# The second feed-forward's input product as seven block products of 256 columns

## The reference

```python
def swiglu(h, w_in, w_out):
    gate, up = jnp.split(h @ w_in, 2, axis=-1)
    return (jax.nn.silu(gate) * up) @ w_out
...
x = x + g2 * swiglu(rms_norm(x, norm_ffn[i]) * (1.0 + sc2) + sh2, ffn_w_in[i], ffn_w_out[i])
```

## Time and profile before

| | us |
|---|---|
| median of the 3 runs shown (2650.46 to 2651.87) | 2650.99 |
| span of the profiled execution | 2648.4 |
| TensorE busy in the span | 2524.9 |
| VectorE, ScalarE, GpSimd busy | 1580.9, 1163.8, 776.8 |
| second feed-forward, from the first full token low part to the end | 2293 to 2648 |

### The profile page before, as it was taken

One profiled execution on the slowest core, in us unless ns is written; L12 is line 12 of the kernel. 1 busy time (PEld: TensorE's weight loads), 2 busy tenths in 40 slices (PEclk: granted clock), 3 DMA queues, 4 the chain that ended last, 5 costly groups with the idle time before them and its releaser, 6 DMA issues.

```text
span 2648.4 us, 41072 instructions
## 1 busy us (share of the span) xinstructions
PE 2524.9 (95%) x15450; PEld 2240.3 (85%) x15450; DVE 1580.9 (60%) x2588; ACT 1163.8 (44%) x2142; POOL 776.8 (29%) x466
## 2 busy tenths in 40 slices
...
GB/s 278 133 143 143 141 174 206 32 70 63 103 96 17 120 76 29 93 122 95 146 142 128 137 87 114 165 101 134 256 205 124 111 33 80 66 98 99 102 96 79
DMA packets 124352, 307.19 MB, mean 116 GB/s; under 512 B 12448, under 2 KB 38048, under 8 KB 122784
## 3 DMA queue, kind: packets, MB, share of 16 engines
...
## 4 chain that ended last, share of the span: by engine, by line
PE 77%; DVE 10%; ACT 5%; issue 5%; POOL 2%; DMA 1%; SPq 0%; ACTq 0%; DVEq 0%; POOLq 0%
PE ps L568 15%; PE ps L570 15%; PE ps L569 15%; PE ps L1627 4%; PE ps L1629 3%; PE ps L1628 3%; PE ps L1522 3%; PE ps L1498 2%; PE ps L1508 2%; ACT prb L2306 1%; PE ps L1402 1%; PE ps L1404 1%; PE ps L1403 1%; PE ps L897 1%; PE ps L936 1%
## 5 line engine op out<-in xcount | busy, mean ns | idle before, releaser
L549 POOL TENSOR_TENSOR Wl<-raws,Wh 128x2048 fp32r<-128x2048 f32 (+3 forms) x82 | 318.6, 3886 | 1200.2 <-ACT Wh L543 1191.3
L568 PE MATMUL ps<-Hh,Wh 128*128 128x384 f32 (+2 forms) x1088 | 375.6, 345 | 6.4 <-DVE xT L3315 2.8
L570 PE MATMUL ps<-Hh,Wl 128*128 128x384 f32 (+2 forms) x1088 | 370.4, 340 | 0.0
L569 PE MATMUL ps<-Hl,Wh 128*128 128x384 f32 (+2 forms) x1088 | 370.3, 340 | 0.0
L543 ACT ACTIVATE Wh<-raws 128x2048 fp32r<-128x2048 f32 (+3 forms) x125 | 204.8, 1639 | 180.2 <-PE ps L570 140.4
L3304 DVE SCALAR_TENSOR_TENSOR xT<-ps,mod,xT 128x384 f32<-128x384 f32 (+3 forms) x174 | 84.5, 533 | 277.8 <-PE ps L570 277.8
L568 PEld LDWEIGHTS ps<-Hh,Wh 128*128 128x128 f32 x1088 | 205.2, 189 | 15.3 <-issue 4.9
L569 PEld LDWEIGHTS ps<-Hl,Wh 128*128 128x128 f32 x1088 | 205.3, 189 | 6.4 <-issue 1.9
L570 PEld LDWEIGHTS ps<-Hh,Wl 128*128 128x128 f32 x1088 | 205.1, 189 | 4.9
L2969 DVE SCALAR_TENSOR_TENSOR ybuf<-ubuf,vec,ybuf 128x770 f32<-128x770 f32 x144 | 155.5, 1080 | 55.1 <-ACT ybuf L1824 40.5
L568 PE MATMUL ps<-H1h,Wh 128*128 128x512 f32 (+1 forms) x368 | 141.7, 385 | 4.5 <-DVE H1l L2844 3.4
...
## 6 DMA issues: line engine op xcount, KB each, us to landing
raws<-in_slabs SPq DMA_DIRECT2D x218, 512.0 KB, 4.6
adl<-in_ada ACTq DMA_DIRECT2D x48, 512.0 KB, 3.6
ada<-in_ada SPq DMA_DIRECT2D x32, 512.0 KB, 3.9
...
ada<-in_ada SPq DMA_DIRECT2D x8, 1024.0 KB, 11.3
...
```

Of the source, the lines that this page charges most:

```text
L549: nc.gpsimd.tensor_tensor(Wl[n % 2][:, 0:w], raw[n % 2][:, 0:w], Wh[n % 2][:, 0:w].bitcast(f32), ALU.subtract).then_inc(sig("slab_lo"), 1)
L568: nc.tensor.matmul(o, lhs(c)[0], rhs(c, t0, t1)[0], start=(s == 0), stop=False)
L569: nc.tensor.matmul(o, lhs(c)[0], rhs(c, t0, t1)[1], start=False, stop=False)
L570: last = nc.tensor.matmul(o, lhs(c)[1], rhs(c, t0, t1)[0], start=False, stop=(s == k - 1))
```

## The change

For chunks 2 to 21 of the second feed-forward the input product takes the seven-product form. The weight slab is cut into quarters: feature blocks 0 to 3 or 4 to 7, gate or up columns. The tokens are cut likewise: feature blocks, and tokens 0 to 255 or 256 to 511. VectorE forms three sums of weight quarters in the tile `gone` and a difference in place (`dve_sums7`), and once the token sums (`dve_tokens7`). A product of the seven is 4 feature blocks x 3 = 12 matmuls on 256 columns. Four of the additions that join the products are left to PSUM: a later product goes on accumulating on a bank that holds an earlier one (`BANK7`; `FRESH7` names the products that start a bank anew). ScalarE copies the state of a bank out before the next product adds to it (`w7_copy`), and VectorE adds gate and up quarters from these copies and from PSUM. Of the seven pieces' low parts GpSimd takes 0, 4, 5 and 6, VectorE 1, 2 and 3. The pieces of one slab fill both slots of `Wh` and `Wl` (0 to 3 in one, 4 to 6 in the other), so each piece of the next slab is written when its predecessor's product is done. Chunks 0 and 1 stay as they were. The loops are written out.

```diff
+        BANK7 = (0, 1, 0, 1, 0, 2, 0)
+        FRESH7 = (0, 1, 5)
...
+        def piece7(t, q):
+            return by_k(t[EVEN7 if q < 4 else 1 - EVEN7][:, 512 * (q % 4):512 * (q % 4) + 512])
...
+        def pe_seven1(pe, grp):
...
+            for y, (x, s, n, c) in enumerate(slabs7(grp)):
+                for q in range(7):
+                    if q in (0, 4, 5):
+                        pe.wait_ge(sig("w7_lo"), past("w7_lo") + 3 * x + (0, 4, 5).index(q) + 1)
+                    elif q < 4:
+                        pe.wait_ge(sig("w7_low"), past("w7_low") + 3 * x + q)
+                    else:
+                        slab_ready(pe, n, 0)
+                    if q == 0 and y == 0:
+                        pe.wait_ge(sig("gemm_evac0"), u0 + s + 1)
+                    if q == 5 and y == 0:
+                        pe.wait_ge(sig("gemm_evac1"), u0 + s + 1)
...
+                    if x == 0 and q in (1, 2, 4, 6):
+                        pe.wait_ge(sig("u7_lo"), past("u7_lo") + (4 if q == 6 else 3))
+                    if q in (2, 3, 4):
+                        pe.wait_ge(sig("w7_copy"), past("w7_copy") + 3 * x + q - 1)
+                    if q == 6:
+                        pe.wait_ge(sig("w7_up"), past("w7_up") + x + 1)
+                    h, l, o = piece7(Wh, q), piece7(Wl, q), ps[:, 3 * (y % 2) + BANK7[q], 0:CTX]
+                    for k in range(4):
+                        th, tl = tokens7(q, k)
+                        nc.tensor.matmul(o, h[:, k, :], th, start=(k == 0 and q in FRESH7), stop=False, skip_group_check=True)
+                        nc.tensor.matmul(o, h[:, k, :], tl, start=False, stop=False, skip_group_check=True)
+                        ins = nc.tensor.matmul(o, l[:, k, :], th, start=False, stop=(k == 3), skip_group_check=True)
+                    ins.then_inc(sig("w7_done" if q < 5 else "gemm_done"), 1)
...
             for grp, n in enumerate(GROUPS[layer]):
-                if layer or not grp:
-                    pe_wide(pe, f"fi{layer}{grp}", KD, hh, hl, w, r=None if grp else 2 * layer + 1)
+                if layer:
+                    if grp == 0:
+                        pe_wide(pe, "fi10", KD, H1h, H1l, w, r=3, only_first=True)
+                    pe_seven1(pe, grp)
...
+        def act_piece7(act, x, s, n, c, q, first):
+            if q in SUM7:
+                act.wait_ge(sig("w7_sum"), past("w7_sum") + 4 * x + q)
+            elif q == 4:
+                act.wait_ge(sig("w7_sum"), past("w7_sum") + 4 * x + 4)
+            else:
+                act.wait_ge(sig(f"slab_in{n % 2}"), 32 * (n // 2 + 1))
+            if first:
+                act.wait_ge(sig("gemm_done"), c - 2 if q < 4 else c)
+            elif q < 5:
+                act.wait_ge(sig("w7_done"), past("w7_done") + 5 * x - 4 + q)
+            else:
+                act.wait_ge(sig("gemm_done"), c + q - 6)
+            nc.scalar.activation(piece7(Wh, q), source7(n, q), ACT.Copy).then_inc(sig("w7_hi" if q < 6 else "slab_hi"), 1)
...
+        def act_seven1(act, grp):
...
+            for y, (x, s, n, c) in enumerate(todo):
+                j, ahead = x % 2, todo[y + 1] if y + 1 < len(todo) else None
+                def next_piece(q):
+                    if ahead:
+                        act_piece7(act, *ahead, q, False)
+                b0 = 3 * (y % 2)
+                for q, (bank, dst) in enumerate(((0, sgb[j]), (1, hdb[j]), (0, None))):
+                    act.wait_ge(sig("w7_done"), past("w7_done") + 5 * x + q + 1)
+                    nc.scalar.activation(mid7[j] if dst is None else dst[:, LAT:T], ps[:, b0 + bank, 0:CTX], ACT.Copy)\
+                        .then_inc(sig("w7_copy"), 1)
+                    next_piece(q)
+                next_piece(3)
+                if not ahead:
+                    act.wait_ge(sig("w7_done"), past("w7_done") + 5 * x + 4)
+                    hi_slab(act, n0f, 0)
+                act.wait_ge(sig("gemm_evac0"), S[f"fi1{grp}"][2] + s + 2)
+                nc.scalar.activation(sgb[j][:, CTX:LAT], sgb[j][:, CTX:LAT], ACT.Silu).then_inc(sig("w7_silu"), 1)
+                next_piece(4)
+                act.wait_ge(sig("gemm_evac1"), S[f"fi1{grp}"][2] + s + 2)
+                nc.scalar.activation(sgb[j][:, 0:CTX], sgb[j][:, 0:CTX], ACT.Silu).then_inc(sig("w7_silu"), 1)
+                next_piece(5)
+                next_piece(6)
+                act.wait_ge(sig("w7_hid"), past("w7_hid") + 2 * x + 2)
+                nc.scalar.activation(G1h[:, s, :], hdb[j][:, 0:LAT], ACT.Copy).then_inc(sig("hid_hi"), 1)
...
+        def act_ffn1(act):
+            n0, ns, u0, c0 = S["fi10"]
+            first = slabs7(0)[0]
+            for jj in range(2):
+                act.wait_ge(sig("gemm_done"), c0 + 2 * jj + 1)
+                nc.scalar.activation(sgb[jj][:, 0:LAT], pairbank(0, LAT), ACT.Silu).then_inc(sig("gemm_evac0"), 1)
+                if jj == 0:
+                    act_tokens7(act, (2, 0, 1))
+                    for q in range(4):
+                        act_piece7(act, *first, q, True)
+                act.wait_ge(sig("gemm_evac1"), u0 + jj + 2)
+                nc.scalar.activation(G1h[:, jj, :], hdb[jj][:, 0:LAT], ACT.Copy).then_inc(sig("hid_hi"), 1)
+            for q in range(4, 7):
+                act_piece7(act, *first, q, True)
+            act.wait_ge(sig("gemm_done"), c0 + 4)
+            act_tokens7(act, (3,))
+            for grp in range(3):
+                act_seven1(act, grp)
+                act_stage(act, f"fo1{grp}", None, prefetch=False)
+                if grp < 2:
+                    for q in range(7):
+                        act_piece7(act, *slabs7(grp + 1)[0], q, True)
...
             pool_stage(pool, "out1", first=1)
+            lo_slab(pool, S["fi10"][0] + 1, 0)
             for grp in range(3):
-                pool_stage(pool, f"fi1{grp}")
-                pool_stage(pool, f"fo1{grp}", prefetch=(grp < 2))
+                for x, s, n, c in slabs7(grp):
+                    for q in (0, 4, 5, 6):
+                        pool_piece7(pool, x, n, q)
+                lo_slab(pool, S[f"fo1{grp}"][0], 0)
+                pool_stage(pool, f"fo1{grp}", prefetch=False)
...
+            a11, a12, a21, a22 = (block7(n, q) for q in (0, 5, 4, 6))
+            if x:
+                dve.wait_ge(sig("w7_low"), past("w7_low") + 3 * x)
+            dve.wait_ge(sig(f"slab_in{n % 2}"), 32 * (n // 2 + 1))
+            nc.vector.tensor_tensor(source7(n, 1), a21, a22, ALU.add).then_inc(sig("w7_sum"), 1)
+            dve.wait_ge(sig("w7_sum"), past("w7_sum") + 4 * x + 1)
+            nc.vector.tensor_tensor(source7(n, 2), source7(n, 1), a11, ALU.subtract).then_inc(sig("w7_sum"), 1)
+            dve.wait_ge(sig("w7_sum"), past("w7_sum") + 4 * x + 2)
+            nc.vector.tensor_tensor(source7(n, 3), a12, source7(n, 2), ALU.subtract).then_inc(sig("w7_sum"), 1)
+            nc.vector.tensor_tensor(a21, a11, a21, ALU.subtract).then_inc(sig("w7_sum"), 1)
...
+        def dve_seven1(dve, grp):
+            todo = slabs7(grp)
+            for y, (x, s, n, c) in enumerate(todo):
+                j, b0 = x % 2, 3 * (y % 2)
+                ahead = todo[y + 1] if y + 1 < len(todo) else None
+                gate, prod = sgb[j], hdb[j]
+                if ahead:
+                    dve_sums7(dve, ahead[0], ahead[2])
+                    dve_low7(dve, ahead[0], ahead[2], 1)
+                    dve_low7(dve, ahead[0], ahead[2], 2)
+                dve.wait_ge(sig("w7_done"), past("w7_done") + 5 * x + 4)
+                dve.wait_ge(sig("w7_copy"), past("w7_copy") + 3 * x + 3)
+                nc.vector.tensor_tensor(gate[:, CTX:LAT], mid7[j], ps[:, b0 + 1, 0:CTX], ALU.add).then_inc(sig("gemm_evac0"), 1)
+                dve.wait_ge(sig("w7_done"), past("w7_done") + 5 * x + 5)
+                nc.vector.tensor_tensor(prod[:, CTX:LAT], prod[:, LAT:T], ps[:, b0, 0:CTX], ALU.add).then_inc(sig("w7_up"), 1)
+                if ahead:
+                    dve_low7(dve, ahead[0], ahead[2], 3)
+                dve.wait_ge(sig("w7_silu"), past("w7_silu") + 2 * x + 1)
+                dve.wait_ge(sig("w7_up"), past("w7_up") + x + 1)
+                nc.vector.tensor_tensor(prod[:, CTX:LAT], prod[:, CTX:LAT], gate[:, CTX:LAT], ALU.mult).then_inc(sig("w7_hid"), 1)
+                dve.wait_ge(sig("gemm_done"), c + 1)
+                nc.vector.tensor_tensor(gate[:, 0:CTX], gate[:, LAT:T], ps[:, b0 + 2, 0:CTX], ALU.add).then_inc(sig("gemm_evac1"), 1)
+                dve.wait_ge(sig("gemm_done"), c + 2)
+                dve.wait_ge(sig("w7_silu"), past("w7_silu") + 2 * x + 2)
+                nc.vector.tensor_tensor(prod[:, 0:CTX], gate[:, 0:CTX], ps[:, b0, 0:CTX], ALU.mult).then_inc(sig("w7_hid"), 1)
+                dve_hidden_low(dve, s, 2 + x, prod)
...
+        def dve_ffn1(dve):
+            n0, ns, u0, c0 = S["fi10"]
+            x, s, n, c = slabs7(0)[0]
+            dve.wait_ge(sig("nq_ld"), 48)
+            dve_tokens7(dve)
+            for jj in range(2):
```

(63 more changed lines are left out.)

49 lines of the change are left out of this document (45 added, 4 removed), and 3 rows, old and new, of the table SHARED.

## The result

The changed kernel took 2660.45 us (median of 6 runs, 2658.5 to 2663.8) against 2650.72 for the kernel before on the same chip: a ratio of 1.0041, 95% interval 1.0029 to 1.0053. It is slower, by 9.7 us (7.7 to 14.0 by that interval); the forecast was 10.0.

What follows compares the result with a forecast made beforehand. TensorE's own work alone bounded the stage; after the change the other engines' loop would. -16.0 + 8.7 + 2.4 + 8.6 + 6.3 = +10.0 us on 2651 gave 2661 us, 2646 to 2671 for 8 in 10.

Steps and rivals of the forecast that it cites:

- TensorE's work: Input product: 84 matmuls of 0.120 us replace 48 of 0.227, 10.08 us a chunk instead of 10.88; -16.0 for 20 chunks.
- the loop: VectorE, ScalarE and GpSimd need 10.7 us a chunk; TensorE waits before the seventh product, 0.62 in 14 chunks: +8.7.
- first chunk of groups 2 and 3: Three more GpSimd low parts stand between VectorE's four sums, so the up addition ends late: 1.2 a chunk, +2.4.
- entry: Start of the stage: VectorE's token sums and ScalarE's queued roundings delay TensorE by 1.6, 2.2, 2.75, 0.9 and 1.2: +8.6.
- seams: Input to output product, three times: first output slab is rounded only after the fourth product; 2.6 twice, 1.1 once: +6.3.
- clock: Rival: TensorE's clock falls at the entry and group ends, four times, +6.8, 2668 us; chance 0.08, nothing in the sum.
- the 2.6 us "around" the span: Runs' median of 2650.99 us less the profiled span of 2648.4, taken as time around the span.
- The rule of the Trainium skill that was weighed there: Weight loads overlap matmuls only on other array rows; a matmul would cost 0.12 + 0.19, the sum 319 us longer.
- TensorE's pace: Rival: VectorE's and GpSimd's turns fall into VectorE's own waits, chunk 10.08, sum -1.1, 2650 us; chance 0.24.
- covered edges: Rival: TensorE's pace with entry and group ends at half, -8.5, 2642.5 us; chance 0.11.

Runs made afterwards that it cites:

- e4: The changed kernel with all seven low parts of the input product on VectorE, none on GpSimd: 2650.7 us, ratio 1.0000.
- e1: The changed kernel with VectorE's gate and up additions moved ahead of low parts 1 and 2: 2677.6 us, ratio 1.0108.
- e2: The changed kernel with low part 1 moved from VectorE to GpSimd: 2672.5 us, ratio 1.0089.
- e3: The changed kernel with the low part of piece 0 moved from GpSimd to VectorE: 2656.5 us, ratio 1.0026.
- e6: e4 with VectorE's and ScalarE's instructions reordered, mainly at the entry to the stage: 2649.3 us, ratio 0.9993.
- e8: e7 with two token sums put behind the hidden product of slab 1, the fourth token rounding behind copy 2, and other entry moves: 2640.4 us, ratio 0.9968.
- e7: e5 with the reordered entry of e6: 2641.6 us, ratio 0.9964.
- e5: e4 with the first output slab of each group rounded and lowered in two halves, TensorE waiting for each separately: 2642.3 us, ratio 0.9966.

## Why the prediction was right, step by step

All in us, for the profiled executions; a loss at a wait is the distance of starts less the 0.12 or 0.227 of an undisturbed matmul.

| term | forecast | measured |
|---|---|---|
| TensorE's work | -16.0 | -16.0: chunks of 10.08 in e4, 10.88 before |
| the loop, 14 chunks | +8.7 | +9.7: 10.77 - 10.08 = 0.69 each |
| first chunk of groups 2 and 3 | +2.4 | +2.3: 1.14 each |
| entry | +8.6 | +6.7: 1.5, 2.1, 2.4, 0.6 |
| seams | +6.3 | +5.9: 2.5, 2.5, 1.0 |
| clock | 0 | +3.1: 1.5 at the entry, 1.6 at the first seam |
| sum | +10.0 | +11.7 (the stage: +12.3) |

The 0.6 between sum and stage is mostly the matmul behind a wait, which starts 0.07 to 0.11 late; the loop's term holds it already. That forecast and median agree to 0.6 us (2661 and 2660.45) is in part luck: the loop cost 1.0 more, the entry 1.9 less and the clock 3.1 more than forecast, and the interval of the measured difference is 6 us wide. One part of the forecast's working is loose: the 2.6 us "around" the span sets a median against one execution (the changed kernel's profiled run has 1.8); the sum doesn't use it.

**TensorE's work.** Right. In e4 the matmuls of all seven products start 0.12 apart for whole chunks. The rule of the Trainium skill that was weighed there ("TensorE: Matmul & The Clock Gate", section "The mechanism" of part 3) does not hold for these instructions. The same section also lets a load for the background weight buffer run ahead, which would allow the 0.12; no run here shows which buffer the loads go to.

**The loop.** Right in mechanism and place, 0.07 a chunk short. Its steps came as forecast, as these rows show. Counted from 2438.70, where sum 1 gets its tiles (its end less 0.54), sum 2 ends at 2.25 where I had 2.27, the up addition at 5.44 for 5.48, GpSimd's low part of piece 5 at 9.05 for 8.97 and of piece 6 at 10.75 for 10.68.

```profile
2437.46 1.78 DVE L3657 TENSOR_TENSOR gone<-raws 128x512 f32<-128x512 f32 x1
2439.28 1.67 DVE L3659 TENSOR_TENSOR gone<-gone,raws 128x512 f32<-128x512 f32 x1
2443.73 0.41 DVE L3689 TENSOR_TENSOR hdb<-hdb,ps 128x256 f32<-128x256 f32 x1
2446.46 1.29 POOL L2880 TENSOR_TENSOR Wl<-raws,Wh 128x512 fp32r<-128x512 f32 x1 [0.22 <-ACT Wh L2337]
2447.71 1.74 POOL L2880 TENSOR_TENSOR Wl<-raws,Wh 128x512 fp32r<-128x512 f32 x1
```

The 0.1 for a wait on two signals, in the loop's upper bound, stands in no row; the whole loop came out 0.07 to 0.09 longer than forecast. e1 to e4 show the mechanism: the chunk's length follows what stands in the turns (11.83, 11.15, 10.39, 10.08) and not what stands ahead of the up addition. In the expectations of e2 and e3 the price of a turn was mis-sized: GpSimd has the tiles for 1.16, but that costs VectorE 0.98. The Trainium skill, "SBUF — State Buffer", section "Who interferes with whom", says that a VectorE instruction with two SBUF inputs contends with a GpSimd instruction that reads SBUF, and that the order of issue decides who blocks; the trace agrees (VectorE's sum takes 1.79 us beside GpSimd and 0.69 without, and GpSimd's low part, 1.38 with next to nothing of VectorE's beside it, takes 1.64 in e1 where it starts while one of VectorE's runs). The Trainium skill, "Perfetto Trace Analysis", section "Optimizing Scalar/DVE Operations", warns that moving work between these two engines might not help; here it did harm, 0.38 us a chunk for each low part on GpSimd in e2 and e3.

**Entry.** Its sum was 1.9 too high. The first two waits came as forecast (1.5 and 2.1 for 1.6 and 2.2), the third at 2.4 for 2.75; the one at q4 (0.9) did not come, and q6's was 0.6 for 1.2. I had derived each from the instruction that stands ahead. e6 to e8 show that a new order mostly moves the waits: their sum is 6.2 us in e4 and 5.0, 3.9 and 6.3 in e6, e7 and e8. That VectorE's total work there sets most of it fits its 28.31 busy us of 29.50 in e8, but no run with less of that work shows it.

**Seams.** Right: 2.5, 2.5 and 1.0, from the rounding that can't start before q3 ends and the 4.55 us low part behind it. e5 shows it by taking them away.

**The clock.** Here the forecast's step failed. I gave it 0.08 as a rival and nothing in the sum, because the waits are 2.75 us and less; no row stood behind that reason. It fell behind two of the three waits of 2.4 to 2.5 us, once to 0.63 over 4 us, where the matmuls start 0.21 apart and not 0.12 (at 1.2 GHz), and cost 3.1. The rival as I put it (four falls, +6.8) did not happen either. That the medians differ by 9.7 and the stages by 12.3 is left open: the falls differ between executions (e2's profile has one behind each of the first two seams, e4's behind the first alone), the time ahead of the stage differs too, and the medians average over both.

**Rivals.** TensorE's pace and covered edges are both out for this kernel (0.46 idle at q6 in every chunk) but they are what e4 and e5 reached, at 2650.7 and 2642.3 where I had put 2650 and 2642.5. e4 got there as the rival had it (chunks of 10.08, entry and seams left); that e5's number fits is luck, since I had put entry and seams at half each, and in e5 the seams are gone and the entry is whole.
